# Hybrid decoder layer: the first two token tiles squared and scaled in halves by two engines, small inputs loaded through another queue

## The reference

```python
def _rmsnorm(x, g):
    x32 = x.astype(jnp.float32)
    y = x32 * lax.rsqrt(jnp.mean(x32 * x32, axis=-1, keepdims=True) + EPS)
    return (y * g.astype(jnp.float32)).astype(x.dtype)

h = _rmsnorm(x, norm_g[l])
proj = jnp.einsum('bsd,de->bse', h, w_in[l])
xa, ga, q, ckv, gb, qi, ki, wi = jnp.split(proj, IN_SPLITS, axis=-1)
# two branches (a gated linear recurrence; sparse attention with a top-256 indexer
# and a relative-position bias) make y
x = x + jnp.einsum('bse,ed->bsd', y, w_out[l])
return _rmsnorm(x, final_norm_g)
```

## Time and profile before

| | |
|---|---|
| median of three executions | 1574.83 us |
| the profiled execution's own time | 1574.92 us |
| its span (first to last instruction) | 1573.0 us, so 1.92 us lie around it |
| PE busy | 1554.3 us, 99% |
| DVE busy | 869.8 us, 55% |
| POOL busy | 642.6 us, 41% |
| ACT busy | 580.7 us, 37% |
| granted clock | 0.999 |

### The profile page before, as it was taken

One profiled execution on the slowest core, in us unless ns is written; L12 is line 12 of the kernel. 1 busy time (PEld: TensorE's weight loads), 2 busy tenths in 40 slices (PEclk: granted clock), 3 DMA queues, 4 the chain that ended last, 5 costly groups with the idle time before them and its releaser, 6 DMA issues.

```text
span 1573.0 us, 20944 instructions
## 1 busy us (share of the span) xinstructions
PE 1554.3 (99%) x7512; PEld 1322.5 (84%) x7512; DVE 869.8 (55%) x1516; ACT 580.7 (37%) x833; POOL 642.6 (41%) x461
## 2 busy tenths in 40 slices
PE   8999999999999999999999999999999999999998
PEld 7799999888888888888888888888887888888886
DVE  6376555588777887878655444487777000040003
ACT  7345555443344444332211111255555122222320
POOL 4354544435545545654444444200001444444640
PEclk9999999999999999999999999999999999999999
DMA  7222111022221222325422222244334623346422
GB/s 273 74 55 74 42 46 40 21 61 84 73 69 52 69 70 83 92 81 170 165 87 87 87 93 80 104 150 154 122 101 148 234 94 99 102 143 258 137 78 107
DMA packets 142528, 163.54 MB, mean 104 GB/s; under 512 B 9494, under 2 KB 106888, under 8 KB 140424
## 3 DMA queue, kind: packets, MB, share of 16 engines
q1 hardware_dynamic: 140936, 158.59, 31.0%
q0 software_dynamic: 1536, 4.20, 0.8%
HBM read 126.58 MB, written 36.18 MB: 103 GB/s over the span
## 4 chain that ended last, share of the span: by engine, by line
PE 96%; DVE 2%; issue 1%; DMA 0%; ACT 0%; DVEq 0%; SPq 0%
PE ps L1200 19%; PE ps L1201 19%; PE ps L1202 19%; PE ps L1452 6%; PE ps L1450 6%; PE ps L1451 6%; PE ps L1438 3%; PE ps L1322 2%; PE ps L1320 2%; PE ps L1421 2%; PE ps L1537 1%; PE ps L1536 1%; PE ps L1535 1%; PE ps L1413 1%; PE ps L1415 1%
## 5 line engine op out<-in xcount | busy, mean ns | idle before, releaser
L1200 PE MATMUL ps<-hT_hi,w_lo 128*128 128x512 f32 (+1 forms) x1344 | 510.7, 380 | 0.0
L1201 PE MATMUL ps<-hT_lo,w_hi 128*128 128x512 f32 (+1 forms) x1344 | 509.2, 379 | 0.0
L1202 PE MATMUL ps<-hT_hi,w_hi 128*128 128x512 f32 (+1 forms) x1344 | 509.2, 379 | 0.0
L800 POOL TENSOR_TENSOR w_lo<-w_raw,w_hi 128x512 fp32r<-128x512 f32 x168 | 236.5, 1408 | 481.3 <-ACT w_hi L892 481.3
L1200 PEld LDWEIGHTS ps<-hT_hi,w_lo 128*128 128x128 f32 x1344 | 252.4, 188 | 43.4
L1201 PEld LDWEIGHTS ps<-hT_lo,w_hi 128*128 128x128 f32 x1344 | 252.4, 188 | 42.9
L1202 PEld LDWEIGHTS ps<-hT_hi,w_hi 128*128 128x128 f32 x1344 | 252.3, 188 | 42.8
L892 ACT ACTIVATE w_hi<-w_raw 128x512 fp32r<-128x512 f32 x168 | 106.0, 631 | 434.2 <-PE ps L1202 303.5
L798 POOL TENSOR_TENSOR w_raw<-w_raw,g_col 128x512 f32<-128x512 f32 x168 | 206.6, 1230 | 36.4 <-DMA w_raw<-in_w_in 36.4
L1892 DVE TENSOR_TENSOR res<-ps,res 128x512 f32<-128x512 f32 x32 | 21.8, 691 | 289.6 <-PE ps L1452 238.9
L828 POOL TENSOR_TENSOR wo_lo<-wo_raw,wo_hi 128x1024 fp32r<-128x1024 f32 x48 | 116.2, 2420 | 153.7 <-ACT wo_hi L1092 153.7
(11 more groups left out here) (217 smaller groups left out, 1904.8 us busy)
## 6 DMA issues: line engine op xcount, KB each, us to landing
w_raw<-in_w_in SPq DMA_DIRECT2D x168, 256.0 KB, 2.8
wo_raw<-in_w_out SPq DMA_DIRECT2D x64, 512.0 KB, 3.7
xin<-in_x SPq DMA_DIRECT2D x8, 1024.0 KB, 7.0
res<-in_x SPq DMA_DIRECT2D x8, 1024.0 KB, 11.2
out<-res SPq DMA_DIRECT2D x16, 512.0 KB, 4.0
y_hi_dram<-y_hi SPq DMA_DIRECT2D x8, 512.0 KB, 2.6
y_lo_dram<-y_lo SPq DMA_DIRECT2D x8, 512.0 KB, 2.7
q_hi_dram<-q_out_hi SPq DMA_DIRECT2D x8, 512.0 KB, 3.7
```

Source lines behind the costliest of these rows:

```text
L800: nc.gpsimd.tensor_tensor(w_lo[:, j, :, :], part, w_hi[:, j, :, :].bitcast(F32), ALU.subtract).then_inc(w_lo_s, 1)
L1200: nc.tensor.matmul(o, wlo, hi, start=(kt == 0), stop=False)
L1201: nc.tensor.matmul(o, whi, lo, start=False, stop=False)
L1202: return nc.tensor.matmul(o, whi, hi, start=False, stop=(kt == KT - 1))
```

## The change

1. The loads of `g_rows`, `rel` and `onehot` are issued from ACT's queue, ahead of ACT's first activation, and no longer from SP's.
2. Tiles 0 and 1 are squared half by ACT (columns 0 to 1023, `half_square`) and half by DVE (columns 1024 to 2047, `half_sum`, a tensor_tensor_reduce). DVE then makes sum / 2048 + EPS of its half, and ACT's root adds it as its bias (`half_root`, which waits for it).
3. Tiles 0 and 1 are scaled in two halves (`norm_half`), and PE turns each half after its own scaling (`x_part`).
4. The order on ACT and DVE around them changes: ACT copies tile 0's first half between tile 1's square and tile 1's root; DVE spreads `rel` before tile 0's square, and its low halves of tile 0 stand between the scalings of tile 1.

Tiles 2 to 7 go as before. The core of the diff:

```diff
-            sp.dma_start(g_rows[:, :], a["norm_g"][0].rearrange("(k p) -> k p", p=P)).then_inc(g_in, 16)
             x_load(0)
             x_load(1)
-            sp.dma_start(rel[:, :], a["rel_bias"]).then_inc(bias_in, 16)
-            sp.dma_start(onehot[:, :], a["onehot"]).then_inc(bias_in, 16)
             x_load(2)
...
+            act.dma_start(g_rows[:, :], a["norm_g"][0].rearrange("(k p) -> k p", p=P)).then_inc(g_in, 16)
+            act.dma_start(rel[:, :], a["rel_bias"]).then_inc(bias_in, 16)
+            act.dma_start(onehot[:, :], a["onehot"]).then_inc(bias_in, 16)
             act.wait_ge(eps_made, 1)
...
+            def half_square(i):
+                act.wait_ge(x_in[i], 16)
+                step.did(nc.scalar.activation(junk[:, 0:D // 2], xin[:, i, 0:D // 2], ACT.Square,
+                                              accum_out=stat[:, i:i + 1]))
+            def half_root(i):
+                act.wait_ge(act_step, i + 2)
+                act.wait_ge(half_mean, i + 1)
+                nc.scalar.activation(stat[:, XB + i:XB + i + 1], stat[:, i:i + 1], ACT.Sqrt, scale=1.0 / D,
+                                     bias=stat[:, 3 * XB + 2 * i + 1:3 * XB + 2 * i + 2]).then_inc(x_sd, 1)
...
-                pe.wait_ge(x_norm, i + 1)
+                if i > 1:
+                    pe.wait_ge(x_norm, i - 1)
                 for j in range(2):
+                    if i < 2:
+                        pe.wait_ge(x_part, 2 * i + j + 1)
                     if i > 0:
                         pe.wait_ge(h_lo, 2 * i - 1 + j)
...
+            def half_sum(i):
+                other = slice(D // 2, D)
+                dve.wait_ge(x_in[i], 16)
+                chain(nc.vector.tensor_tensor_reduce(junk[:, D // 2:D], xin[:, i, other], xin[:, i, other],
+                                                     1.0, 0.0, ALU.mult, ALU.add,
+                                                     stat[:, 3 * XB + 2 * i:3 * XB + 2 * i + 1]))
+                nc.vector.tensor_scalar(stat[:, 3 * XB + 2 * i + 1:3 * XB + 2 * i + 2],
+                                        stat[:, 3 * XB + 2 * i:3 * XB + 2 * i + 1], 1.0 / D, EPS, ALU.mult, ALU.add
+                                        ).then_inc(half_mean, 1)
+            def norm_half(i, j):
+                part = slice(j * D // 2, (j + 1) * D // 2)
+                nc.vector.tensor_scalar(xin[:, i, part], xin[:, i, part], stat[:, 2 * XB + i:2 * XB + i + 1], None, ALU.mult
+                                        ).then_inc(x_part, 1)
```

More of the change, by code:

```diff
@@ L380, in layer @@
         x_in = [sem(f"x_in{i}") for i in range(XB)]
+        half_sq = sem("half_sq")
+        half_mean = sem("half_mean")
+        x_part = sem("x_part")
         x_rest = [sem(f"x_rest{i}") for i in range(QB - XB)]
@@ L878, in root_x, with high_half @@
                                      scale=1.0 / D, bias=eps[:, :]).then_inc(x_sd, 1)
+            def high_half(i, j):
+                act.wait_ge(x_tp, 2 * i + j + 1)
+                nc.scalar.activation(
+                    hT_hi[:, 8 * j:8 * j + 8, i * P:(i + 1) * P],
+                    X[j][:, :].rearrange("p (t s) -> p t s", s=P), ACT.Copy).then_inc(h_hi, 1)
             def high_x(i):
                 for j in range(2):
[L882 to L885, removed]
+                    high_half(i, j)
             def high(t, js=range(PIECES)):
@@ L897, in _ @@
             act.wait_ge(act_step, s)
[L898 to L901, removed]
+            def half_square(i):
[7 more added lines that the diff above has]
+                                     bias=stat[:, 3 * XB + 2 * i + 1:3 * XB + 2 * i + 2]).then_inc(x_sd, 1)
+            half_square(0)
+            half_root(0)
+            half_square(1)
+            high_half(0, 0)
+            half_root(1)
+            high_half(0, 1)
             for i in range(QB):
-                high_x(i)
+                if i > 0:
+                    high_x(i)
                 if i + 2 < QB:
@@ L1564, in _, with invert @@
             nc.vector.tensor_copy(g_col[:, :], X[0][:, 0:KT]).then_inc(g_made, 1)
+            def half_sum(i):
[7 more added lines that the diff above has]
+                                        ).then_inc(half_mean, 1)
+            def invert(i):
+                dve.wait_ge(x_sd, i + 1)
+                chain(nc.vector.reciprocal(stat[:, 2 * XB + i:2 * XB + i + 1], stat[:, XB + i:XB + i + 1]))
+            def norm_half(i, j):
+                part = slice(j * D // 2, (j + 1) * D // 2)
+                nc.vector.tensor_scalar(xin[:, i, part], xin[:, i, part], stat[:, 2 * XB + i:2 * XB + i + 1], None, ALU.mult
+                                        ).then_inc(x_part, 1)
             def norm_x(i):
@@ L1571, in norm_x, with low_half @@
                                         ).then_inc(x_norm, 1)
+            def low_half(i, j):
+                dve.wait_ge(h_hi, 2 * i + j + 1)
+                part = (slice(None), slice(8 * j, 8 * j + 8), slice(i * P, (i + 1) * P))
+                tt(hT_lo[part], X[j][:, :].rearrange("p (t s) -> p t s", s=P),
+                   hT_hi[part].bitcast(F32), ALU.subtract).then_inc(h_lo, 1)
             def low_x(i):
                 for j in range(2):
[L1575 to L1581, removed]
+                    low_half(i, j)
+            dve.wait_ge(bias_in, 32)
+            nc.vector.tensor_copy(rel_wide[:, :, :], rel[:, :].rearrange("b (h o) -> b h o", o=1).broadcast_to(
+                [BUCKETS, NH, COPIES])).then_inc(rel_made, 1)
+            half_sum(0)
+            invert(0)
+            norm_half(0, 0)
+            norm_half(0, 1)
+            half_sum(1)
+            low_half(0, 0)
+            invert(1)
+            norm_half(1, 0)
+            low_half(0, 1)
+            norm_half(1, 1)
+            for i in range(1, QB):
                 if i + 1 < QB:
                     norm_x(i + 1)
[L1584 to L1587, removed]
                 if i == 3:
```

## The result

The changed kernel takes 1581.44 us (median of seven, 1578.81 to 1582.08), the kernel before, beside it, 1574.89 (median of seven, 1574.57 to 1576.93). The ratio is 1.0034, with a 95% interval of 1.0024 to 1.0044, all of it above 1.002: slower, and outside the range I gave (1573.6 to 1577.0). The profiled execution is the fastest of the seven, 1578.81 with a span of 1576.9, 3.9 us longer than before.

What follows compares the result with a forecast made beforehand. PE bounds the kernel, and DVE's order bounds its start (turn 2, then turn 3). Gains of 0.26 us at turn 2 and 0.1 at turn 3, summed as 0.35, gave 1574.5 us, range 1573.6 to 1577.0.

Steps and rivals of the forecast that it cites:

- x earlier by 0.46: SP's queue: without g_rows's issue, x's first issue moves from 1.21 to 0.75, tile 0 lands at 5.75, not 6.21.
- ACT's issues and table load, hidden: ACT's start: three issues end at 3.1, the table load at 4.4, covered by the wait for tile 0 until 5.75.
- g_rows lands at 3.1: ACT's queue: g_rows lands 1.6 us after issue, at 3.1, not 2.35; WARM ends at 9.35, starting turn 0.
- WARM rival: PE's start: WARM ends after 9.35; one us late gives 1575.5, the bound of 3.0 gives 1577.5; chance 0.25.
- onehot lands at about 5: ACT's queue: onehot, issued at 2.42, lands between 4.0 and 9.0, taken as about 5.
- bias rival: DVE's start: late onehot holds tile 0's square; landing at 9.0 puts turn 0 at 12.6, 3.25 later, 1577.8; chance 0.12.
- The rule on taking turns: DMA engines: each alternates between queues with work, a packet each, so small loads on another queue pass big ones.
- The added squares cost nothing: DVE: the added 2 x (1.22 + 0.2) us lie in waiting time, with about 1.1 us of cover.
- DVE's chain: DVE ahead of turn 2: low half 0 at 11.52, tile 1's at 16.72 instead of 16.98; turn 2 at 18.08, gain 0.26.
- a scaling of 1.54: Tile 3's scaling before turn 3: 1.54 against the usual 1.29, taken as not repeating; about 0.1 us regained there.
- PE's clock: PE's gap between turns 0 and 1: 2.6 us against 2.48 before, which did not make turn 1 slow.
- clock rival: PE's gap between turns 0 and 1: clock falls, 1.5 to 3 us lost, about 1576.5; chance 0.05.

Runs made afterwards that it cites:

- e14: Changed kernel with DVE's bias_in wait and rel_wide copy behind tile 1's square, PE's gaps filled with unread transposes: 1578.69 us, ratio 1.0022.
- e13: Changed kernel with g_rows back at the head of SP's queue, PE's gaps filled with unread transposes, 20 more in WARM: 1577.34 us, ratio 1.0012.
- e12: e6 with WARM placed ahead of the transposition of g_rows: 1578.33 us, ratio 1.0020.
- e5: e2 with unread identity transposes in PE's gaps (20 behind turn 0, 6 inside turn 1, 4 ahead of turn 2): 1575.27 us, ratio 0.9999.
- e9: e5 with POOL's first work on the key weights held until tile 2 is scaled: 1575.78 us in one execution.
- e10: Kernel before with 20 unread transposes behind turn 0 and 4 ahead of turn 2: 1574.94 us against 1575.93, ratio 0.9996.
- e6: Changed kernel with unread identity transposes in PE's gaps, the same filling as e5: 1578.37 us, ratio 1.0019.
- e2: Changed kernel with the three small loads back in SP's queue, rel_wide copied behind DVE's square of tile 1: 1577.63 us, ratio 1.0010.
- e8: Changed kernel with tiles 0 and 1 loaded as four loads of 512 columns each: 1579.49 us in one execution.
- e1: Kernel before with only g_rows, rel and onehot issued on ACT's queue: 1579.13 us against 1575.4, ratio 1.0026.
- e4: Changed kernel with DVE's rel_wide copy and bias_in wait moved behind the square of tile 1: 1581.03 us, ratio 1.0030.
- e11: e10 with DVE's bias_in wait and rel_wide copy moved between the scalings of tiles 0 and 1: 1574.63 us against 1575.93, ratio 0.9994.

## Why the prediction was wrong

By its own steps:

- *x earlier by 0.46:* right. First issue at 0.75, tile 0 there at 5.73 (forecast 5.75).
- *ACT's issues and table load, hidden:* right. 1.49 to 2.97, table load 3.00 to 4.28, 1.2 us of wait left.
- ***g_rows lands at 3.1:* the step that failed first.** I took the 1.6 us of an empty queue, where the transfer engines had been empty too. It took 5.5, WARM ended at 12.7 instead of 9.35. In the sum this delay stood at nothing; with the clock held up it is worth 3.4 us (e14). The WARM rival, at 0.25, named just this: g_rows sharing the transfer engines with the tiles, each us of delay a us on turn 0. But its price was one us; its bound of 3.0 us was the array's late rise, another cause, and g_rows's own delay, 3.9 us, was not bounded at all. That bound's 1577.5 also lay outside the range, which the prediction does not say where it names the cases that the range leaves out.
- ***onehot lands at about 5:* failed likewise.** 6.4 from its issue, at 8.8. The bias rival named this mechanism, its queue on DVE and its landing (9.0) rightly, at 0.12; it priced 3.25 us where e13 shows 2.1, and it was not exclusive with the WARM rival, as I had treated it. Both came at once in the changed kernel. Its 12.6 for turn 0 is close to the measured 12.69 by luck: by bias_in alone turn 0 would have stood at 11.93 (e12), most of the difference being the copy of rel_wide, 0.21 where I had 0.7, and 12.69 is WARM's end.
- *The rule on taking turns.* In "Queues, rings and completion order" of "DMA: Bandwidth & Descriptors" the Trainium skill has each transfer engine take turns between the queues, a packet each, and a packet there is typically about 9 to 17 descriptors. I had read a packet as small beside a load. Tile 0's share on one engine is eight pieces of 8 KB and a semaphore write, so by this rule it can be one packet, and g_rows behind it fits. Tile 1's share is just as large, and there the trace does not agree: 61 packets of ACT's queue moved by 7.0, before tile 1 was through. I let the rule weigh against the bias rival; it had no number for this case either way.
- *The added squares cost nothing:* right in e5, where DVE's two squares took 1.22 to 1.23 us and ended before the first low half at 11.24 (forecast 11.5). In the changed kernel itself everything stood later, the square of tile 1 (12.36) took 1.74 beside POOL, and it still ended 0.5 us before the first low half could start.
- *DVE's chain, 5.20 us from low half 0 to the low half of tile 1 (11.52 to 16.72):* 6.17 in e5 (11.24 to 17.41), 0.97 longer. The start, 0.28 earlier than forecast, should have put turn 2 before 18.08; the chain took that back and 0.69 more. The terms mis-sized are the second scaling of tile 1 (1.34 from start to next start, where I had 0.66) and tile 2's (1.47, where I had 1.24), 0.9 us together, both beside POOL's work. Turn 2: forecast 18.08, e5 18.77, e9 17.98. The earlier trace rows had the sign of it, a scaling of 1.54, which I took as not repeating.
- ***PE's clock:* the second step that failed.** I gave it 0.05 because a gap of 2.48 us had been harmless in the one profile of before. PE's gaps were not harmless in many unprofiled executions of the same kernel (e10), and I had taken their spread (1574.57 to 1576.24) for noise. In the sum the clock stood at nothing. In the changed kernel it costs from 0.4 us (1578.8 against e6's 1578.4) to 3.7 (1582.08), at the median 3.1; in e2, with the loads in place, 2.4. The clock rival forecast 1.5 to 3 us for it, so its size was about right and its chance too low.

The sum, in medians: 1574.5 forecast, 0.8 for POOL beside DVE (e5), 3.1 for the late loads (e6), 3.1 for the clock, 1581.4 measured. The first of these terms is e5 minus a forecast and so holds the forecast's other small errors too. The terms come from different batches, and the median of the kernel before differs between batches by up to 1.0 us (1574.89 to 1575.93), as more or fewer of its executions had the low clock; the filled kernels don't have that spread.

What stays open: what exactly lets the clock fall. The empty time between turns 0 and 1 was 2.48 us before, 2.52 in e2 and 2.71 in the changed kernel, so its length alone doesn't divide them; e2's clock fell at 13.9, after turn 0, that gap and the first transposes of turn 1, and the changed kernel's at 17.1, still inside the gap. That filling the gaps keeps it up is shown; which gap matters most was not tried. Open too is why the small loads passed nothing of tile 0 and yet took turns with tile 1.

## What to carry to other kernels

A small load on a second DMA queue is not ahead of a big load issued before it: here nothing of it moved until 1 MB of x was nearly through. What others wait for should be issued before the first big load; at the head of SP's queue g_rows took 1.6 us. Cutting the big load helped g_rows less, 3.5 us, and made the big load itself 2.2 us later (e8). A warm-up on PE hides delays only as long as it starts early and ends where the real work begins; make its start depend on nothing that is loaded, and let it reach up to the work. The first without the second won nothing (e12); both together were not run. And where a kernel's executions differ by a tenth of a per cent, look at the granted clock of each before calling the spread noise: here it told that PE's gaps, harmless in one profile, were not in other executions.

## What the runs showed of the hardware

- The same 8 KB load took 1.6 us from issue to landing with idle transfer engines, on SP's queue or on ACT's, 3.5 behind quarters of a tile (256 KB each), 5.0 to 5.5 behind whole tiles of 1 MB on the other queue (e1, e4, e6, e12, e14 and the changed kernel). Of the two tiles issued ahead of it, it landed after the first (5.7) and before the second (8.7).
- WARM's 36 transposes took 5.58 to 7.07 us in different profiles (7.07 in e4, 6.78 in e11, 5.62 in e12), by where in it the array rises to its upper level: seven transposes took 1.75 us at its start and twelve 1.47 later on the earlier trace rows. The profile's rows print a granted clock of 1.00 for the slow part too, so there only the pace shows the level. Ahead of idle time WARM's length is free; in the changed kernel, e1, e4, e6 and e14 it is on the path.
- A DVE scaling of 128x1024 float32 took 0.75 us with POOL idle and 1.42 beside POOL's two-source subtraction; a 32x128 copy with a repeated operand 0.21 and 0.74.
